# Masks of the gated delta rule made inside the block inverse before it, and six fp32 products turned into three-pass products

## The reference, cut to what matters

```
# block 1
y_conv = cb * dwconv(cc * cx)
y_na   = neighbourhood_attention(nq, nk, nv, rpb)      # 4 heads of 64, bias from rpb
y_gdn  = gated_delta_chunked(...) forward + backward   # 4 heads of 128, chunks of 64
mixed  = concat([y_conv, y_na, y_gdn]) @ w_out         # 1024 x 1024
x      = x + gate1 * mixed;  x = x + gate2 * hier_moe(...)   # 32 experts
# gated delta rule, per chunk
diff   = g[..., :, None] - g[..., None, :]             # g: cumulated log decay
lower  = (kb @ k.T) * exp(where(strict, diff, -inf))
intra  = (q @ k.T) * exp(where(incl, diff, -inf))
sol    = triangular_solve(I + lower, [v * beta, kb * exp(g)])
# block 2
y_a = u * (spatial(layer_norm(v)) + b_s);  y_b = hgrn recurrence, gated
x   = alpha * x + ((y_a @ w_a) * sig(ga) + (y_b @ w_b) * sig(gb)) @ w_o
# block 3
y_conv = silu(layer_norm(conv31(...))) @ conv_w_out + conv_b_out
y_att  = causal difference attention, 8 heads
y      = (g_conv * y_conv + g_att * y_att) @ w_o;   then w_ff1, relu squared, w_ff2
```

## Time and profile before

| | us |
|---|---|
| median of 3 runs | 3724.31 (3723.46 to 3726.82) |
| the profiled execution's own time | 3726.51 |
| its span in the trace | 3724.6 |
| PE busy | 3312.6 (89%) |
| DVE busy | 1811.9 (49%) |
| ACT busy | 1243.9 (33%) |
| mean granted clock of PE | 0.926 of full speed |

### The profile page before, as it was taken

How to read it: one execution, slowest core, us unless ns; L and a number is a source line. 1 busy time by engine, 2 the same in 40 slices (tenths; PEclk the granted TensorE clock), 3 DMA queues, 4 the chain that set the end, 5 groups by cost and what they waited for, 6 DMA issues and landing times.

```text
span 3724.6 us, 34562 instructions
## 1 busy us (share of the span) xinstructions
PE 3312.6 (89%) x13568; PEld 2320.0 (62%) x13568; DVE 1811.9 (49%) x2689; ACT 1243.9 (33%) x1864; POOL 44.4 (1%) x76
## 2 busy tenths in 40 slices
PE   7987678789999976899899899999799978969997
PEld 3644676467667653658664378877577755438786
DVE  5335554256566544513562145554598855133343
ACT  2215113255555533215242122222422254032233
POOL 0000000000000000000000000000000000000000
PEclk9998889889999997999899999999899966989999
DMA  8420001379999962212013125541122210103220
GB/s 287 153 96 1 1 1 65 140 293 385 384 379 390 376 252 101 91 68 91 23 46 113 62 76 190 189 151 62 43 79 88 91 68 1 68 23 113 79 79 23
DMA packets 146798, 486.12 MB, mean 131 GB/s; under 512 B 8176, under 2 KB 11888, under 8 KB 134128
## 3 DMA queue, kind: packets, MB, share of 16 engines
q1 hardware_dynamic: 130544, 438.58, 31.6%
q10 hardware_dynamic: 10368, 24.79, 1.7%
q0 software_dynamic: 5760, 20.97, 1.4%
HBM read 459.15 MB, written 25.17 MB: 130 GB/s over the span
## 4 chain that ended last, share of the span: by engine, by line
PE 83%; DVE 8%; ACT 4%; issue 3%; DMA 1%; SPq 0%; POOL 0%; POOLq 0%; ACTq 0%; DVEq 0%; PEldq 0%
PE bank L456 15%; PE bank L458 14%; PE bank L457 14%; PE bank L355 14%; PE bank L1603 5%; PE bank L1114 3%; PE bank L2182 2%; PE bank L553 2%; PE bank L2766 2%; PE bank L545 1%; PE bank L2788 1%; PE bank L1571 1%; DMA ring<-in_w_ada 1%; PE bank L2776 1%; PE bank L2626 0%
## 5 line engine op out<-in xcount | busy, mean ns | idle before, releaser
L457 PE MATMUL bank<-h_parts,A_parts 128*128 128x512 f32 x1424 | 561.3, 394 | 0.0
L355 PE MATMUL bank<-A,ring 128*128 128x512 f32 x800 | 350.0, 600 | 15.1 <-DVE A L1260 8.4
L456 PE MATMUL bank<-h_parts,A_parts 128*128 128x512 f32 x816 | 323.4, 396 | 35.9 <-DVE h_parts L2984 13.4
L458 PE MATMUL bank<-h_parts,ring_parts 128*128 128x512 f32 x848 | 333.8, 394 | 0.0
L445 ACT ACTIVATE A_parts<-ring 128x1024 fp32r<-128x1024 f32 x162 | 170.4, 1053 | 420.9 <-PE bank L458 420.1
L457 PEld LDWEIGHTS bank<-h_parts,A_parts 128*128 128x128 f32 x1424 | 271.7, 191 | 58.6 <-issue 3.8
L452 DVE TENSOR_TENSOR ring_parts<-ring,A_parts 128x1024 fp32r<-128x1024 f32 x162 | 198.0, 1223 | 205.4 <-ACT A_parts L445 205.4
L355 PEld LDWEIGHTS bank<-A,ring 128*128 128x128 f32 x800 | 153.9, 193 | 209.4 <-issue 193.0
L1642 DVE TENSOR_TENSOR ring_parts<-ring,h_parts 128x1024 fp32r<-128x1024 f32 x192 | 225.7, 1221 | 42.7 <-ACT h_parts L1705 41.9
L458 PE MATMUL bank<-h_parts,A_parts 128*128 128x512 f32 x576 | 227.6, 395 | 0.0
L456 PE MATMUL bank<-A_parts 128*128 128x512 f32 x544 | 214.8, 395 | 5.3 <-DVE A_parts L2492 5.2
(11 more groups left out here) (493 smaller groups left out, 5398.5 us busy)
## 6 DMA issues: line engine op xcount, KB each, us to landing
ring<-in_expert_w SPq DMA_DIRECT2D x64, 2048.0 KB, 9.3
ring<-in_w_in SPq DMA_DIRECT2D x37, 2048.0 KB, 7.9
A<-in_expert_w SPq DMA_DIRECT2D x32, 2048.0 KB, 9.4
ring<-in_w_ada SPq DMA_DIRECT2D x24, 2048.0 KB, 12.4
ring<-in_w_ff SPq DMA_DIRECT2D x16, 2048.0 KB, 7.6
slot_rows<-A ACTq DMA_DIRECT2D x32, 512.0 KB, 9.2
ring<-in_w_ffn_gate SPq DMA_DIRECT2D x5, 2048.0 KB, 7.7
ring<-in_w_ffn_up SPq DMA_DIRECT2D x5, 2048.0 KB, 7.9
```

The source lines that it names most:

```text
L355: mm = pe.matmul(bank[tile % 4][:], ring_tile(g)[:, k, m * P:(m + 1) * P], rhs(k), start=(k == 0), stop=(k == g.kt - 1))
L456: pe.matmul(out, parts(w_high), parts(r_low), start=start, stop=False)
L457: pe.matmul(out, parts(w_high), parts(r_high), start=False, stop=False)
L458: return pe.matmul(out, parts(w_low), parts(r_high), start=False, stop=stop)
```

## The change

Delta rule: the ten mask operations of a direction become nine (the constants `near_f`, `near_b`, `far_f`, `far_b` hold the strict mask as well), and the masks of block b+1 are issued between the steps of block b's inverse: PE's row products behind step 1 and its dot products behind steps 2 and 3, ACT's exponentials behind step 3, DVE's stages 2 to 10 one behind each of the steps 2 to 10, for both directions. Block 0's masks come beforehand, both directions by turns. `bias_dve` goes from behind `in_dve` into it, and the attention's first wait changes with it.

Six products become `project_split`. `high_of` (ACT) and `low_of` (DVE) split their activations: for `out` in scan steps 1 to 4 (first four tiles) and in `gdn_out` (last four), with two weight slices in scan steps 5 and 6; for `wa2` behind each spatial tile, whose bias now comes from an extra one-row matmul instead of a DVE addition; for `wb2` behind each gate tile; for `wo2` and `wo3` behind each merged tile; for `co3` inside attention units 0 to 8, two weight slices in units 8 to 10. Five expert loads wait until `out` is done (two were issued earlier), the ring slots of `co3` and `wo3` change, and the first two loads of ff1 wait for the last tile of `wo3`.

```diff
+        def high_of(act, dst, src):
+            return act.activation(parts(dst), src, ACT.Copy)
+        def low_of(dve, t, high):
+            return dve.tensor_tensor(parts(t), t, parts(high), ALU.subtract)
...
+            bias_dve(dve)
...
+            pe.wait_ge(sem("tile_read"), L["xq_in"][0].first_tile + 4)
...
+        def mask_dots_pe(pe, b, i):
             c = slice(b * P, (b + 1) * P)
-            dve.tensor_tensor(A[:, 4 + 4 * d:8 + 4 * d, c], A[:, 12:16, c], heads(e_row), ALU.mult)\
-                .then_inc(signal("masks_done"), 1)
-        def gdn_masks_act(act, b, d):
+            for j in range(GH):
+                mm = pe.matmul(head(bank[1 - i][:], j), W(16 + j)[:, c], W((12, 16)[i] + j)[:, c], start=True, stop=True)
+            mm.then_inc(sem("mask_dots"), 1)
...
+        def mask_dve(dve, b, stage, step):
+            for d in range(2):
+                n = 2 * b + d
+                diff, incl = W(44 + d), W(22 + d)
+                b4 = lambda ap: spread(ap[:, b, 4 * d:4 * d + 4], P, at=2)
+                if stage == 2:
+                    dve.wait_ge(*seen("g_rows", n + 1))
+                    ins = dve.tensor_tensor(heads(diff), heads(bank[2 + d][:]), b4(g_cum), ALU.subtract)
+                elif stage == 3:
+                    dve.tensor_scalar(diff, diff, 0.0, None, ALU.min).then_inc(signal("g_diff"), 1)
+                elif stage == 4:
+                    dve.wait_ge(*seen("decay", n + 1))
+                    ins = dve.tensor_tensor(heads(incl), heads(diff), spread(sq(INC[d]), GH), ALU.mult)
+                elif stage == 5:
+                    dve.wait_ge(sem("mask_dots"), 2 * b + 1)
+                    dve.tensor_tensor(h[:, 4 * d + b, :], incl, bank[1][:], ALU.mult).then_inc(signal("intra"), 1)
+                elif stage == 6:
+                    dve.wait_ge(sem("mask_dots"), 2 * b + 2)
+                    ins = dve.tensor_tensor(diff, diff, bank[0][:], ALU.mult)
+                elif stage == 7:
+                    ins = dve.tensor_tensor(heads(diff), heads(diff), b4(beta), ALU.mult)
+                elif stage == 8:
+                    dve.wait_ge(*seen("intra", n + 1))
+                    ins = dve.tensor_tensor(heads(incl), heads(diff), spread(sq(NEAR[d]), GH), ALU.mult)
+                elif stage == 9:
+                    dve.tensor_tensor(heads(W(46 + d)), heads(diff), spread(sq(FAR[d]), GH), ALU.mult)\
+                        .then_inc(signal("masks_done"), 1)
+                elif stage == 10:
+                    dve.wait_ge(*seen("row_exp", n + 1))
+                    c = slice(b * P, (b + 1) * P)
+                    dve.tensor_tensor(A[:, 4 + 4 * d:8 + 4 * d, c], A[:, 12:16, c], heads(W(20 + d)), ALU.mult)\
+                        .then_inc(sem("row_used"), 1)
...
+                if 1 <= i <= 4:
+                    dve.wait_ge(sem("mixed_high"), i)
+                    low_of(dve, W(MIXED[i - 1]), mixed_high(i - 1)).then_inc(sem("mixed_split"), 1)
+                if 5 <= i <= 6:
+                    split_low(dve, out_slices[i - 5], out_high)
...
+            def mixed_low(n):
+                dve.wait_ge(sem("mixed_high"), n + 1)
+                low_of(dve, W(MIXED[n]), mixed_high(n)).then_inc(sem("mixed_split"), 1)
...
+                if j:
+                    mixed_low(3 + j)
+            mixed_low(7)
...
-            pe.wait_ge(*seen("y_gdn", GH))
-            pe.wait_ge(*seen("na_out", len(units)))
-            project(pe, L["out"], lambda k: W(MIXED[k]))
+            project_split(pe, out_slices, out_high, mixed_high, lambda k: W(MIXED[k]),
+                          first=lambda k: pe.wait_ge(sem("mixed_split"), k + 1))
+        def out_act(act):
+            for s in out_slices[2:]:
+                split_high(act, s, out_high)
...
+                if j + 2 < len(out_slices):
+                    split_low(dve, out_slices[j + 2], out_high)
...
-            sp.wait_ge(*seen("y_gdn", GH))
-            for s, j in ((1, 0), (0, 2)):
-                load(j, s, mats[j][s])
...
-            for s, j in ((0, 0), (0, 1), (1, 2)):
+            for s, j in ((0, 0), (0, 1), (1, 0), (0, 2), (1, 2)):
...
+            mask_rows_pe(pe, 0)
+            mask_dots_pe(pe, 0, 0)
+            mask_dots_pe(pe, 0, 1)
             for b in range(TT):
-                gdn_masks_pe(pe, b)
                 for k in range(1, 11):
                     for d in range(2):
                         inverse_pe(pe, b, d, k)
+                    if b + 1 < TT:
+                        if k == 1:
+                            mask_rows_pe(pe, b + 1)
+                        if k in (2, 3):
+                            mask_dots_pe(pe, b + 1, k - 2)
...
-            bias_dve(dve)
             na_dve(dve)
+            ada_dve(dve, L["ada11"][0], 16, 48, col("b_ada", 0, 48), ((1, col("norm_ffn_w", 0, 8)),), "ada_rest")
             gdn_norm_dve(dve)
             step = ordered(dve, "masks_dve")
+            for stage in range(2, 11):
+                mask_dve(dve, 0, stage, step)
             for b in range(TT):
-                for d in range(2):
-                    gdn_masks_dve(dve, b, d, step)
                 for k in range(1, 11):
                     for d in range(2):
                         inverse_dve(dve, b, d, k, step)
+                    if k >= 2 and b + 1 < TT:
+                        mask_dve(dve, b + 1, k, step)
...
-                    pe.wait_ge(*seen("spatial_added", g - 1))
+                    pe.wait_ge(*seen("y_a", g - 1))
                 for t in range(TT):
-                    mm = pe.matmul(bank[4 + g % 2][:, t * P:(t + 1) * P], v_tok(t)[:, g * P:(g + 1) * P], spatial(g),
-                                   start=True, stop=True)
+                    c = slice(t * P, (t + 1) * P)
+                    pe.matmul(bank[4 + g % 2][:, c], sq("ones")[0:1, :], head(row2(2), g)[0:1, :], start=True, stop=False)
+                    mm = pe.matmul(bank[4 + g % 2][:, c], v_tok(t)[:, g * P:(g + 1) * P], spatial(g),
+                                   start=False, stop=True)
                 mm.then_inc(signal("spatial_mixed"), 1)
-            pe.wait_ge(*seen("y_a", KD))
-            project(pe, L["wa2"], lambda k: W(8 + k))
+            project_split(pe, wa_slices, gm_high, y_high, lambda k: W(8 + k),
+                          first=lambda k: pe.wait_ge(sem("y_a_split"), k + 1))
...
-                t4 = W(42 + g % 2)
-                then(dve.tensor_tensor(heads(t4), heads(bank[4 + g % 2][:]), spread(head(row2(2), g), TT), ALU.add),
-                     "spatial_added")
-                dve.wait_ge(*seen("spatial_added", g + 1))
-                dve.tensor_tensor(W(8 + g), W(8 + g), t4, ALU.mult).then_inc(signal("y_a"), 1)
+                dve.tensor_tensor(W(8 + g), W(8 + g), bank[4 + g % 2][:], ALU.mult).then_inc(signal("y_a"), 1)
+                if g:
+                    y_low(g - 1)
+            y_low(KD - 1)
+            for s in gm_slices[18:26]:
+                split_low(dve, s, gm_high)
...
-            pe.wait_ge(*seen("y_b", HH))
-            project(pe, L["wb2"], lambda k: W(24 + k))
-            pe.wait_ge(*seen("merged", KD))
-            project(pe, L["wo2"], W)
+            project_split(pe, wb_slices, wbo_high, lambda k: W(8 + k), lambda k: W(24 + k),
+                          first=lambda k: pe.wait_ge(sem("y_b_split"), k + 1))
+            project_split(pe, wo_slices, wbo_high, lambda k: W(16 + k), W,
+                          first=lambda k: pe.wait_ge(sem("merged_split"), k + 1))
...
+                low_of(dve, W(24 + j), W(8 + j)).then_inc(sem("y_b_split"), 1)
...
+            for s in wbo_slices[:2]:
+                split_low(dve, s, wbo_high)
             for j, tile in enumerate(tiles_of(*L["wb2"])):
+                split_low(dve, wbo_slices[j + 2], wbo_high)
...
+                high_of(act, W(8 + j), W(24 + j)).then_inc(sem("y_b_high"), 1)
+                if j >= HH - 2:
+                    split_high(act, wbo_slices[j - (HH - 2)], wbo_high)
...
+        for g in L["ff1"][:2]:
+            g.also = ("tile_ready", L["wo3"][-1].first_tile + 4)
...
+                if u < KD:
+                    act.wait_ge(*norm_at("conv_ln", "out", u + 1))
+                    high_of(act, conv_high(u), W(16 + u)).then_inc(sem("conv_high"), 1)
+                elif u < KD + 2:
+                    split_high(act, coo_slices[u - KD], coo_high)
...
+                if 1 <= u <= KD:
+                    dve.wait_ge(sem("conv_high"), u)
+                    low_of(dve, W(15 + u), conv_high(u - 1)).then_inc(sem("conv_split"), 1)
+                elif KD < u <= KD + 2:
+                    split_low(dve, coo_slices[u - KD - 1], coo_high)
...
-            pe.wait_ge(*norm_at("conv_ln", "out", KD))
+            pe.wait_ge(sem("conv_split"), KD)
             pe.wait_ge(*seen("att", 8 * TT))
-            project(pe, L["co3"], lambda k: W(16 + k))
-            pe.wait_ge(*seen("merged3", KD))
-            project(pe, L["wo3"], W)
```

(3 more changed lines are left out.)

153 lines of the change are left out of this document (105 added, 48 removed).

## The result

The changed kernel takes 3636.4 us in the median (3633.0 to 3638.1); against the kernel before the ratio is 0.9762, interval 0.9745 to 0.9779, so 87.6 us less. I had forecast 3611 and 113 less. The one large miss lies at the spatial mixing of block 2; it is 32.7 us, and some 7 us on the other side, mostly at the difference attention, make the total look better than it is.

What follows compares the result with a forecast made beforehand. PE was taken to bound the kernel, busy 89% of the span. The terms summed to -113.3: from 3726.51 profiled to 3613.2, and 3611 as the median lies 2.2 lower; range 3583 to 3648.

Steps and rivals of the forecast that it cites:

- Neighbourhood attention, -10: Ahead of the neighbourhood attention: DVE's bias work moves into idle time, -8.8, and PE not idling gives about 1 more.
- Delta rule, -43.5: Delta rule: masks inside the inverse save 38.7 us over three blocks, 3.8 at the opening, 1 in the last block.
- my walk: Delta rule, one block step by step: 31.9 us, plus 0.9 for seams makes 32.8, against 45.7 before.
- Rival C: Delta rule runs at 1.2 GHz, 54.6 us of work a block, about +42 there; total 3697, chance 0.05.
- `out`: Product behind the scan: in three passes, starting before its last operand is whole, it ends at 678.2 against 691.3; -13.
- `wb2` and `wo2`: Block 2's later products in three passes: -7 for `wb2`, starting 3.3 us late, and -12.4 for `wo2`.
- `co3` and `wo3`: Block 3's products around the end of the difference attention, in three passes: -11.4 for `co3` and -12.5 for `wo3`.
- rival B: Six products: hand-offs eat the three passes' gain of 66.8 us; total 3678, chance 0.07.
- rival E: Six products: the split chain becomes serial, 9.3 us a tile, 183 more than forecast; total 3794, chance 0.04.
- `wa2` with the spatial mixing, -10.5: Block 2: mixing with the one-row bias matmul takes 16 us, three-pass product 43.6, ending at 1632.2 against 1642.7.
- Difference attention, +6.5: Block 3's attention: low parts add 0.65 us in each of eight units, weight slices 0.65 to 0.8 twice.
- Rival D: Block 3's attention leaves 1.2 GHz, or leaves it earlier, giving back 24 us; total 3587, chance 0.10.

Runs made afterwards that it cites:

- experiment 7: Kernel before (3724) with only the bias table's work moved into `in_dve` and `ada_rest` put behind the attention: 3710.6 us, ratio 0.9945.
- experiment 6: Kernel before (3724) with only the delta rule's part of the change, all products fp32, bias table where it was: 3681.2 us, ratio 0.9879.
- experiment 2: Changed kernel with the spatial bias matmul over all 128 rows (identity times bias rows) instead of one row: 3604.2 us, ratio 0.9668.
- experiment 4: Changed kernel with nine extra fp32 matmuls of 128x512 into an unused bank while PE idles ahead of the spatial stage: 3629.7 us, ratio 0.9733.
- experiment 5: Changed kernel with the spatial bias matmul over 64 rows instead of one, so it computes another result: 3633.5 us in one run.
- experiment 9: Changed kernel with spatial bias on DVE again, v's four norms ahead of two late slice splits, and `wb2` slice splitting earlier: 3594.8 us, ratio 0.9640.
- experiment 11: Kernel with spatial bias on DVE and mended DVE order (3583.9 us), difference attention's scores over 128 rows, computing another attention: 3556.7 us, ratio 0.9546.
- experiment 12: Kernel with spatial bias on DVE and mended DVE order (3583.9 us), scores over 128 rows, POOL copying each head into zero-padded tiles: 3553.1 us, ratio 0.9539.
- experiment 8: Changed kernel with the conv outputs' and first two `co3` weight slices' splitting moved from attention units 0 to 10 to behind the attention: 3641.4 us, ratio 0.9773.

## Why the prediction was right, and where it was wrong

**Neighbourhood attention, -10: 10.1, in part by luck.** PE's first scores come at once and DVE takes them up at 263.93, 16.48 us after its last work, waiting for PE and not for the bias:

```profile
263.93 0.69 DVE L881 SCALAR_TENSOR_TENSOR A<-bank,A 128x512 f32<-128x512 f32 x1 [16.48 <-PE bank L830]
```

So the bias is off the path as forecast. But how long PE stays at 1.2 GHz behind that varies: the traces of the other kernels that are alike up to there have 6.9 to 10.5 us at the same point, and experiment 7's has 5.3.

**Delta rule, -43.5: right, 47.** The mechanism is the one forecast, and experiment 6 shows it alone. The period is 31.49 against my walk's 31.9 before I added 0.9 for seams; there was nothing to add. Opening 3.5, forecast 3.8; last block 0.9, forecast 1. Rival C (1.2 GHz here) is out: 1.00, with matmuls that all use 128 rows.

**The six products.** `out` -13.3 against -13; `wb2` and `wo2` together -17.6 against -19.4; `co3` and `wo3` -23.2 against -23.9. So rivals B and E are out: inside the six products PE waited for no weight slice, and only three times 0.3 us for the low part of the last activation. The one hand-off that I had priced (3.3 us at `wb2`) is there, piece by piece, in the chain:

```profile
1952.95 0.69 ACT A L2513
1953.63 0.53 ACT A_parts L521
1954.18 0.69 DVE A_parts L524
1954.87 1.15 DVE ring_parts L452
1956.07 0.80 PE bank L456
```

**`wa2` with the spatial mixing, -10.5: wrong, +22.2.** The step that failed is the price of the one-row matmul: "about 2 x 0.89 per feature tile (priced as a product of the delta rule)". It is 5.8 us per feature tile (8 matmuls of 0.72). I took the duration of a matmul from its columns and type and left out its rows. The Trainium skill ("TensorEngine Tiling (Array Packing)", Key Properties) says that changing the tiling mode drains PE; it gives no price, and it does not say whether a matmul over part of the rows is such a change. These traces show a price at each change of rows. Experiments 2, 4 and 5 show what the rows do: 64 matmuls of 0.22 would be 14 us; at full clock 64 changes between all and part of the rows would add 12.5, which makes 64 x 0.415 = 26.6; the other 19.4 are the clock, which the alternation brings to 1.2 GHz and keeps there. (At 1.2 GHz a change costs 0.28 to 0.295 us instead of 0.19.) My upper bound for the term, twice my value, was too near as well: 46 is nearly three times 16. Correcting this term alone (32.7 us) gives 3611 + 33 = 3644 against 3636. That the time still fell into my range is partly luck: the attention's error gave back 7.3 of it, and with that attention as in experiments 4 and 9, 12 us longer, the time would have been 3648, the edge of the range.

**What the trace of before had to say on it.** In the attention's row of 0.50 at a PE busy for 32.90 of 38 us I saw only that being busy is no warrant for the clock. I did not ask which matmuls stand there: scores over 64 of 128 rows, between others over 128. Experiments 11 and 12 show that without these 64-row matmuls the clock comes back in these units; since 11 has no rows of zeros, it isn't the zeros that do it. Of the clock, the Trainium skill ("TensorE: Matmul & The Clock Gate", Part 1: The HAM clock gate) says that it depends on how busy PE has recently been; in the changed kernel's spatial mixing PE counts as busy for 46.07 of 46.10 us and is granted 0.50. For these rows the sentence does not hold if one reads "busy" off the profile.

**What the rows do not explain.** Matmuls over 64 rows between ones over 128 do not always bring 1.2 GHz. The neighbourhood attention has them too, one score matmul over 64 rows a unit between turns and mixes over 128, and runs at full clock (timeline of PE and a window, changed kernel):

```profile
287.28 1.09 PE L850 MATMUL bank<-A 128*64 128x128 f32 x8
288.30 1.12 PE L830 MATMUL bank<-A 64*128 64x512 f32 x2
289.35 0.66 PE L838 MATMUL bank<-square,A 128*128 128x128 f32 x4
```

```profile
285.00:306.00 21.00, 20.51 (x115) 12.42 (x114) 15.13 (x33) 13.26 (x33) 0.00 (x0) 1.00 0.00 1
```

In experiment 7's trace the clock even rises in the midst of them: it is at 0.50 from 272 to 282 and at 1.00 from 283 to 312. The last units of the difference attention run at full clock as well, with 64-row scores. What tells these stretches from the others no experiment here shows.

**Difference attention, +6.5: wrong, -0.8.** I priced a low part at 0.65 because one unit showed 0.17 us of DVE idling. The window over nearly nine such units in the trace of before shows more:

```profile
3012.00:3030.00 18.00, 17.38 (x55) 12.38 (x55) 14.35 (x64) 12.61 (x59) 0.00 (x0) 0.50 0.54 201
```

DVE is busy for 14.35 of 18 us, so 0.4 are free in a unit of 2.06. The units became 0.38 longer (2.44 from start to start), 1.8 us were left of it from unit 8 on, and the clock came back 2 us earlier at the end. Experiment 8 puts the whole at 2.4.

**Rival D (the attention leaves 1.2 GHz)** did not happen in the changed kernel, but it is real: by 12 us between traces of kernels that are alike there (experiment 9), and by 28 to 30 where the rows are changed.

## What to carry to other kernels

Price a matmul by its rows too: one that uses part of the rows, in turn with ones that use all, costs at each change and can hold PE at 1.2 GHz (in two stretches of this kernel it did, in the neighbourhood attention it didn't), even where it seems to do almost nothing. Where a stretch shows PE busy and the clock at 0.50, look for such matmuls first; padding with zeros from an idle engine gave back 28 us here. And read idle time per unit from a window over many units, not from one row.

## What the runs showed of the hardware that I had not expected

- fp32 matmuls of 128 columns with 128 rows: 0.22 us each; in turn with ones of 1 row: 0.415 at full clock, 0.72 at half; in turn with ones of 64 rows 0.72 at half, too.
- The granted clock fell from 1.00 to 0.50 in the midst of such an alternation without a gap on PE, 3.7 us after its start (experiment 4).
- Matmuls over 64 rows between ones over 128 ran at 0.50 in most of the difference attention and at 1.00 in the neighbourhood attention.
- The same units of the difference attention took 27.0 us at 0.94 or 38.8 at 0.63, in kernels that are alike there. Comparisons of 0.3% between kernels with such a stretch need several runs or a trace up to it.
